# Which partitions the rows of an expert's 64-row block lie in

## The chip, the cores and the metric

One core of one Trainium2 chip. The metric is device time in microseconds (us) of one execution, the median of several. The kernel before takes 1628.13 us (three runs, 1624.47 to 1629.79). TensorE is called PE in the profile, VectorE DVE, ScalarE ACT, GpSimd POOL, SyncE SP; "SPq" and "POOLq" are their instruction queues, where DMAs are issued.

## The reference

Two transformer blocks run one after the other on 512 tokens of width 1024. The first is attention (global and dilated) and a convolutional feed-forward layer, the second a state-space scan beside windowed attention, and then a mixture of experts. Only the mixture matters here:

```python
expert = g_idx * EXPERTS_PER_GROUP + e_idx          # top 2 of 8 experts in the top 1 of 4 groups
...
def expert_block(args):
    xb, e = args
    return (jax.nn.silu(xb @ w_gate[e]) * (xb @ w_up[e])) @ w_down[e]
...
out = jax.ops.segment_sum(y_buf.astype(f32) * w_buf[:, None], tok_buf, num_segments=n_tok + 1)
```

Each of 512 tokens goes to 2 of 32 experts, so an expert has 32 tokens on the average, and which ones is known only on the device. An expert's weights are three matrices of 1024 x 512, 1024 x 512 and 512 x 1024 in float32, 2048 KB each, 6 MB together; 32 experts are 192 MB, all of them read once. The order of an expert's tokens among its rows has no part in the result.

## The kernel before

The mixture of experts begins at about 1036 us (the last norm and the router) and its loop over experts at about 1108 us. The rest of the kernel isn't touched by the change.

**The tables.** The router gives each of the 1024 (token, expert) pairs a block (the expert's own first block of `BLK` = 64 rows, or a later block if it has more than 64) and a rank `pk` in that block, 0 to 63, without gaps. DVE compares `pk` with the constant row `C("place")` (L2223) to make `hot_p`, one column for each partition; PE multiplies it with `hot_b` (L1638), and the product is, for each block and each partition, the number of the token that lies there and its weight (`tok_of`, `place_weight`, L2239 to L2242). A partition in which nobody lies gets an index above the last token.

**The gather.** For expert n, POOL copies column n of `tok_of` to `tok_at` (L916) and issues an indirect DMA (L920). It reads row `tok_at[p]` (4096 bytes) of the normed tokens, which were stored to device memory before, into partition p of `xg`, for the 64 partitions p = 0 to 63. Where the index is out of bounds the row is left out. `xg` has two buffers; the gather of expert n waits until PE has transposed the rows of expert n - 2 out of the same buffer (`xt_filled`), and its rows are wanted at the transposes of expert n, two turns later.

**The turn of an expert.** PE transposes the 64 rows (L1654), DVE scales them (L2249, L2252), PE multiplies by gate and up (L1668, 16 steps over two halves), transposes the hidden rows, and multiplies by down (L1688). The result is split in a high and a low part and added to the tokens by a matmul with a 0/1 matrix `spread` (L1703). `spread` is made by DVE (L2276, L2278): the key of a pair, 64 times its block plus its rank, is compared with `C("slot")`, which says which key a partition holds. All matmul helpers are recorded at L1289, transposes at L1292.

**The weights.** SP streams them through two sets of three slots, `arena` for even and `ring` for odd experts, by one 2048 KB DMA each (`load_expert`, L764). Gate and up of expert n + 2 are issued when PE has done gate and up of expert n; down of expert n + 2 when down of expert n is done. At the time of its issue a load has others ahead of it in the same queue. The loads are all on SP's queue (q1 in the profile), the gathers on POOL's (q0), and both are served by the core's 16 DMA engines. One load is 128 partitions of 16 KB, 8 packets of 16384 bytes for each DMA engine.

Of the kernel before, what the change touches and what calls it, by code (L numbers as in the profile page):

```python
# [14 lines left out]
P = 128  # L15
# [12 lines left out]
BLK = 64  # L28
NOVF = 2 * T // BLK - 1
NBLK = E + NOVF  # L30
# [9 lines left out]
def constants():  # L40

    f = np.float32
    i = np.arange(P)
    col = i[:, None]
    row = i[None, :]
    t = {}
    t["ident"] = np.eye(P, dtype=f)
    t["eps"] = np.full((P, 1), EPS, f)
    t["zero"] = np.zeros((P, 1), f)
    t["upto"] = (col <= row).astype(f)  # L50
    t["from"] = (col >= row).astype(f)
    t["before"] = (col < row).astype(f)
    t["one"] = np.ones((P, 1), f)
    t["window"] = np.concatenate([np.where(row >= col, 0, BIG), np.zeros((P, P)), np.where(row <= col, 0, BIG),
                                  np.zeros((P, CTX))], axis=1).astype(f)
    tok = np.arange(T)
    r, c = (tok // 64).astype(f)[:, None], (tok % 64).astype(f)[:, None]

    def tiles(a):
        return a.reshape(TT, P, -1).transpose(1, 0, 2).reshape(P, -1).astype(f)  # L60

    inv = (f(10000.0) ** (-np.arange(0, 32, 2, dtype=f) / f(32))).astype(f)[None]
    ar, ac = r * inv, c * inv
    rope1 = tiles(np.concatenate([np.cos(ar), np.cos(ar), np.cos(ac), np.cos(ac)], 1)), tiles(np.concatenate(
        [-np.sin(ar), np.sin(ar), -np.sin(ac), np.sin(ac)], 1))
    inv = (f(10000.0) ** (-np.arange(16, dtype=f) / f(16))).astype(f)[None]
    a = np.concatenate([r * inv, c * inv], 1)
    t["cos2"] = tiles(np.concatenate([np.cos(a), np.cos(a)], 1))
    t["sin2"] = tiles(np.concatenate([-np.sin(a), np.sin(a)], 1))
    t["low"] = (i < 64).astype(f)[:, None]  # L70
    t["high"] = (i >= 64).astype(f)[:, None]
    e = np.arange(E)
    t["expert"] = np.tile(e, (P, 1)).astype(f)
    t["group"] = np.tile(e // EG, (P, 1)).astype(f)
    t["blocks_on"] = np.tile(E - 1 - e, (P, 1)).astype(f)
    t["block"] = np.tile(np.arange(NBLK), (P, 1)).astype(f)
    t["place"] = np.tile(np.arange(BLK), (P, 1)).astype(f)
    t["full_blocks"] = np.tile(BLK * np.arange(1, T // BLK), (P, 1)).astype(f)

    t["both_halves"] = (i[:, None] % 64 == np.arange(E + E // EG)[None]).astype(f)  # L80

    t["numbers"] = np.repeat(tok.reshape(TT, P).T + 1, 2, axis=1).astype(f)
    t["slot"] = (np.arange(NBLK)[None] * BLK + (i % BLK)[:, None]).astype(f)
    at, out = {}, []
    for k, v in t.items():
        at[k] = (sum(x.shape[1] for x in out), v.shape[1])
        out.append(v.astype(f))
    return at, np.ascontiguousarray(np.concatenate(out, axis=1)), np.ascontiguousarray(np.concatenate(rope1, axis=1))
# [70 lines left out]
def two_blocks(nc, consts_d, rope1_d, dist_d, h_d, inp, out):  # L159
    ctx = ExitStack()  # L160
    with ctx:
        cols, _, _ = constants()
        ncols = sum(w for _, w in cols.values())

# [2179 lines left out]
```

How the kernel before makes its waits and increments, by code:

```python
    def wait(self, eng, key):  # L112
        eng.wait_ge(self.sem, self.at[key])
# [8 lines left out]
    def link(self, eng, ins):  # L122
        self.n += 1
        ins.then_inc(self.sem, 1)
        eng.wait_ge(self.sem, self.n)
# [26 lines left out]
    def filled(self, eng, key):  # L152
        n = self.at[key]
        eng.wait_ge(self.sems[n % 8], n // 8 + 1)
        return self.banks[n % 8]
# [598 lines left out]
        def load_expert(sp, e, par, kpar, reuse, only=range(3)):  # L754
            for i, (name, pat) in enumerate((("w_gate_2", "a e (p j) f -> (a e) p (j f)"),
                                             ("w_up_2", "a e (p j) f -> (a e) p (j f)"),
                                             ("w_down_2", "a e (p f) d -> (a e) p (f d)"))):
                if i not in only:
                    continue
                kw = {"f": 4} if i == 2 else {"j": KT}
                if reuse is not None:
                    sp.wait_ge(gu_filled if i < 2 else y_filled, reuse)
                sp.dma_start(EXPERT_SLOTS[3 * par + i], inp[name].rearrange(pat, **kw)[e]).then_inc(
                    expert_in[3 * par + i], 16)
# [12 lines left out]
        def columns(sp, first):  # L778
            if first:
                sp.wait_ge(row_stored, 16 * ROWS_BEFORE[6])
                for c in range(2):
                    sp.dma_start(mod[:, c, 0:2, :], h_d[6 * c:6 * c + 2, :].rearrange("s (p j) -> p s j", j=KT)).then_inc(
                        mod_in, 16)
# [4 lines left out]
        @block.sync  # L789
# [36 lines left out]
            route_pe.wait(sp, "halves")
            sp.wait_ge(h_stored, 16)
            sp.wait_ge(expert_in[0], 16)
```

## Time and profile before

| | before |
|---|---|
| median of 3 runs | 1628.13 us |
| profiled execution, its own time | 1627.91 us |
| its span | 1626.1 us |
| PE busy | 1468.7 us (90%) |
| DVE busy | 918.7 us (56%) |
| q1 (SP's DMA queue) | 296.33 MB, 48.8% of 16 engines' span |
| q0 (POOL's DMA queue) | 3200 packets, 7.87 MB, 1.5% |

"Share" of a DMA queue is the time that its packets took, divided by 16 engines times the stretch; it can pass 1 a little, since packets overlap at their ends. In the packet line of the DMA view the counts "under 512 B", "under 2 KB" and "under 8 KB" each hold the ones before. A gathered row is one packet of 4096 bytes, so in a stretch with nothing else of that size the number of rows is the count under 8 KB less the count under 2 KB. A place left empty is a packet of 4 bytes on q0, and so is the end mark of each engine; a gather has 64 + 16 = 80 packets on q0. The end marks of the weight loads are 4-byte packets on q1.

### The profile page before, as it was taken

How to read it: one execution, taken by the hardware profiler on the slowest of the kernel's cores; microseconds unless marked ns; L12 is line 12 of the kernel's file. 1: busy time of each engine (PE TensorE's matmuls, PEld its weight loads, DVE VectorE, ACT ScalarE, POOL GpSimd, SP SyncE). 2: the span in 40 equal slices, each digit the busy share in tenths (PEclk: the TensorE clock that was granted, in tenths of full speed). 3: DMA queues.
4: the chain of work that ended last, by engine and by line, in shares of the span. 5: the costliest groups of instructions: out<-in, count | busy, mean ns of one | idle time of the engine just before them, and what ended most of it. 6: DMA issues, size and time to landing. Idle time of an engine off the chain costs nothing. (4 is left out here: it accounts for less than half of the span.)

```text
span 1626.1 us, 20275 instructions
## 1 busy us (share of the span) xinstructions
PE 1468.7 (90%) x7799; PEld 1018.5 (63%) x7799; DVE 918.7 (56%) x1701; ACT 516.8 (32%) x938; POOL 99.4 (6%) x132
## 2 busy tenths in 40 slices
PE   6899996999999989989998897948998989898896
PEld 5676665788777778877877686734444444343443
DVE  4845774467787667753664676372344344444435
ACT  4435665343353332243426544221111101010102
POOL 0000000000000000001003122001001001000100
PEclk9999997999999999999999998978999999999998
DMA  7222011155444358603010000564999999999993
GB/s 225 78 78 72 1 47 52 52 180 144 140 132 129 95 177 272 209 29 128 26 62 18 1 2 1 207 259 152 406 401 410 416 408 412 398 411 401 410 410 134
DMA packets 103146, 308.33 MB, mean 190 GB/s; under 512 B 12959, under 2 KB 64511, under 8 KB 89739
## 3 DMA queue, kind: packets, MB, share of 16 engines
q1 hardware_dynamic: 93424, 296.33, 48.8%
q0 software_dynamic: 3200, 7.87, 1.5%
q10 hardware_dynamic: 6427, 2.84, 0.7%
q8 instruction: 63, 1.03, 0.3%
q14 instruction: 32, 0.26, 0.1%
HBM read 306.99 MB, written 4.22 MB: 191 GB/s over the span
## 5 line engine op out<-in xcount | busy, mean ns | idle before, releaser
L1289 PE MATMUL bank<-weights_high,hT_high 128*128 128x512 f32 (+2 forms) x736 | 257.6, 388 | 18.6 <-DVE hT_low L1782 5.2
L1289 PE MATMUL bank<-weights_low,hT_high 128*128 128x512 f32 (+2 forms) x560 | 214.8, 384 | 0.0
L1746 DVE TENSOR_TENSOR weights_low<-ring,weights_high 128x2048 fp32r<-128x2048 f32 (+2 forms) x61 | 135.7, 2224 | 137.6 <-ACT weights_high L953 136.7
L953 ACT ACTIVATE weights_high<-ring 128x2048 fp32r<-128x2048 f32 (+2 forms) x61 | 113.4, 1860 | 202.7 <-PE bank L1289 157.2
L1289 PEld LDWEIGHTS bank<-weights_high,hT_high 128*128 128x128 f32 x736 | 140.3, 191 | 47.1 <-issue 11.2
L1289 PE MATMUL bank<-hT_high,weights_high 128*128 128x512 f32 x416 | 164.2, 395 | 1.6 <-DVE hT_low L1784 1.6
L1289 PE MATMUL bank<-hT_low,weights_high 128*128 128x512 f32 x416 | 163.1, 392 | 0.0
L1289 PE MATMUL bank<-hT_high,weights_low 128*128 128x512 f32 x416 | 161.8, 389 | 0.0
L2249 DVE TENSOR_TENSOR hTc<-bank,mod_gain 128x512 f32<-128x512 f32 x32 | 22.1, 691 | 229.2 <-PE bank L1292 229.2
L1289 PE MATMUL bank<-arena,hTc 128*64 128x512 f32 x496 | 117.7, 614 | 21.8 <-DMA arena<-in_w_up 20.2
L1289 PE MATMUL bank<-ring,hTc 128*64 128x512 f32 (+1 forms) x544 | 120.8, 582 | 13.3 <-DMA ring<-in_w_up 13.3
L1289 PEld LDWEIGHTS bank<-weights_low,hT_high 128*128 128x128 f32 x560 | 106.9, 191 | 20.4 <-issue 0.2
L1289 PEld LDWEIGHTS bank<-ring,hTc 128*64 128x64 f32 (+1 forms) x544 | 46.5, 140 | 86.1 <-issue 85.0
L1289 PEld LDWEIGHTS bank<-arena,hTc 128*64 128x64 f32 x496 | 42.1, 141 | 91.5 <-issue 91.5
L1292 PEld LDWEIGHTS bank<-const,xn 64*128 64x128 f32 (+1 forms) x464 | 62.3, 203 | 57.9 <-issue 45.7
L1292 PE MATMUL bank<-const,xn 64*128 64x64 f32 (+1 forms) x464 | 67.7, 301 | 30.6 <-DVE xn L1766 19.6
L1289 PEld LDWEIGHTS bank<-hT_high,weights_high 128*128 128x128 f32 x416 | 78.2, 188 | 22.1 <-issue 3.4
L1256 ACT ACTIVATE hTc<-bank 128x512 f32<-128x512 f32 x32 | 19.1, 597 | 222.6 <-PE bank L1289 222.6
L1289 PEld LDWEIGHTS bank<-hT_high,weights_low 128*128 128x128 f32 x416 | 78.1, 188 | 17.3
L1292 PE MATMUL bank<-const,arena 128*128 128x128 f32 x429 | 71.5, 294 | 18.7 <-ACT arena L1072 6.2
L1289 PEld LDWEIGHTS bank<-hT_low,weights_high 128*128 128x128 f32 x416 | 78.1, 188 | 16.4
L1289 PE MATMUL bank<-weights_high,hT_low 128*128 128x512 f32 (+1 forms) x224 | 85.3, 381 | 0.0
(324 smaller groups left out, 2328.4 us busy)
## 6 DMA issues: line engine op xcount, KB each, us to landing
arena<-in_w_up SPq DMA_DIRECT2D x16, 2048.0 KB, 23.3
arena<-in_w_down SPq DMA_DIRECT2D x16, 2048.0 KB, 21.6
ring<-in_w_gate SPq DMA_DIRECT2D x16, 2048.0 KB, 18.4
ring<-in_w_up SPq DMA_DIRECT2D x16, 2048.0 KB, 23.5
ring<-in_w_down SPq DMA_DIRECT2D x16, 2048.0 KB, 22.4
arena<-in_w_gate SPq DMA_DIRECT2D x15, 2048.0 KB, 18.2
xn<-in_w_ada SPq DMA_DIRECT2D x48, 512.0 KB, 5.0
ring<-in_w_up SPq DMA_DIRECT2D x44, 512.0 KB, 5.1
```

The lines of the kernel that those rows point to most:

```text
L953: high_ready.tick(s.activation(part_view(w_high, key), raw_view(key), ACT.Copy), k)
L1256: s.activation(gu[:, par, :], ps[1][:, :], ACT.Copy).then_inc(gu_ready, 1)
L1289: return nc.tensor.matmul(o, lhsT, rhs, start=start, stop=stop)
L1292: return nc.tensor.transpose(o, i, ident[0:n, 0:n])
L1746: low_ready.tick(v.tensor_tensor(part_view(w_low, key), raw_view(key), part_view(w_high, key), ALU.subtract), k)
L2249: v.tensor_tensor(xT[:, par, :, :], ps[0][:, :].rearrange("p (j n) -> p j n", j=KT), wide(mod_gain[:, 2, :], BLK), ALU.mult).then_inc(xt_s ...
```

## The change

Only constants change. `held[p]` is the rank that partition p holds. Before it is p itself; now it is 16 (p mod 4) + p // 4. So rank r lies in partition 4 (r mod 16) + r // 16: ranks 0 to 15 in partitions 0, 4, 8, ... 60, ranks 16 to 31 in 1, 5, ... 61, and so on. `place` (which rank a partition takes when the table is made) and `slot` (which key a partition has when results are spread) both follow it, so each row is still found where it lies. No instruction, shape or wait is added, removed or moved.

```diff
-    t["place"] = np.tile(np.arange(BLK), (P, 1)).astype(f)
+    held = np.arange(BLK) % 4 * (BLK // 4) + np.arange(BLK) // 4
+    t["place"] = np.tile(held, (P, 1)).astype(f)
...
-    t["slot"] = (np.arange(NBLK)[None] * BLK + (i % BLK)[:, None]).astype(f)
+    t["slot"] = (np.arange(NBLK)[None] * BLK + held[i % BLK][:, None]).astype(f)
```

## Rows read from the trace of the kernel before

**Rows 1.** Waits in 1110 to 1600 us: who waited for whom: us in total, times, longest
```profile
PE bank L1289 <- DMA arena<-in_w_up: 20.2, 12, 3.1
PE bank L1289 <- DMA ring<-in_w_up: 13.3, 11, 2.0
```

**Rows 2.** The chain that ended last, in order of time: start us, us, what
```profile
1178.29 12.50 PE bank L1289 x64
...
1192.50 12.53 PE bank L1289 x64
...
1205.62 23.20 DMA arena<-in_w_up
...
1571.64 21.60 DMA ring<-in_w_up
...
1593.38 7.10 PE bank L1289 x32
```

**Rows 3.** Busy time by stretch; the last two numbers are DMA share and GB/s
```profile
1110.00:1150.00 40.00, 37.61 (x166) 14.68 (x166) 9.33 (x16) 3.90 (x8) 3.56 (x6) 0.89 0.70 263
1150.00:1205.00 55.00, 55.00 (x293) 23.56 (x291) 26.41 (x43) 5.77 (x11) 5.38 (x7) 1.00 1.01 407
1205.00:1400.00 195.00, 177.86 (x939) 82.66 (x940) 83.53 (x136) 20.32 (x38) 18.03 (x26) 0.99 1.01 409
```

**Rows 4.** The same view where the weight stream runs out
```profile
1576.00:1578.00 2.00, 2.00 (x12) 0.57 (x8) 1.54 (x3) 0.00 (x0) 0.00 (x0) 1.00 1.00 426
...
1588.00:1590.00 2.00, 2.00 (x18) 1.15 (x16) 1.94 (x5) 0.00 (x0) 0.00 (x0) 1.00 0.92 393
1590.00:1592.00 2.00, 2.00 (x13) 0.59 (x10) 1.97 (x4) 0.00 (x0) 0.00 (x0) 1.00 0.81 344
1592.00:1594.00 2.00, 1.63 (x10) 0.52 (x8) 0.95 (x2) 0.16 (x1) 0.00 (x0) 1.00 0.52 221
1594.00:1596.00 2.00, 2.00 (x12) 0.72 (x10) 0.69 (x1) 0.47 (x1) 0.00 (x0) 1.00 0.31 131
```

**Rows 5.** DMA view, 1126.1 to 1127.5 us (queue: packets, MB, share of 16 engines)
```profile
DMA packets 114, 0.39 MB, mean 278 GB/s; under 512 B 73, under 2 KB 73, under 8 KB 96
...
q0 software_dynamic: 80, 0.09, 18.8%
```

**Rows 6.** DMA view, 1448.84 to 1449.25 us: the first 0.41 us of a gather
```profile
DMA packets 19, 0.16 MB, mean 400 GB/s; under 512 B 3, under 2 KB 3, under 8 KB 11
...
q0 software_dynamic: 11, 0.03, 20.4%
```

**Rows 7.** DMA view, 1450.50 to 1454.0 us: the later part of that gather
```profile
DMA packets 137, 1.39 MB, mean 398 GB/s; under 512 B 52, under 2 KB 52, under 8 KB 52
```

**Rows 8.** DMA view, 1448.84 to 1453.5 us: that gather whole
```profile
DMA packets 196, 1.75 MB, mean 376 GB/s; under 512 B 74, under 2 KB 74, under 8 KB 94
```

**Rows 9.** DMA view, a larger gather: 1496.82 to 1498.85, then 1498.85 to 1501.3
```profile
DMA packets 77, 0.66 MB, mean 327 GB/s; under 512 B 11, under 2 KB 11, under 8 KB 45
...
DMA packets 96, 0.85 MB, mean 348 GB/s; under 512 B 38, under 2 KB 38, under 8 KB 46
```

**Rows 10.** DMA view, 1496.82 to 1501.9 us: the same gather whole
```profile
DMA packets 190, 1.78 MB, mean 350 GB/s; under 512 B 50, under 2 KB 50, under 8 KB 92
...
q0 software_dynamic: 80, 0.17, 10.4%
```

**Rows 11.** DMA view, 1384.0 to 1389.5 us: the largest gather
```profile
DMA packets 187, 1.79 MB, mean 325 GB/s; under 512 B 36, under 2 KB 36, under 8 KB 92
```

**Rows 12.** DMA view, first and last of 26 gathers: from 1168.8, from 1561.1, 5.5 us each
```profile
DMA packets 222, 2.15 MB, mean 391 GB/s; under 512 B 78, under 2 KB 78, under 8 KB 95
...
DMA packets 213, 2.04 MB, mean 370 GB/s; under 512 B 73, under 2 KB 73, under 8 KB 94
```

**Rows 13.** The instructions on token_index
```profile
L920 POOL DMA_INDIRECT xn<-normed_tokens,token_index x32: 962/1207/1281, 1103.3 to 1556.8; - x32
...
DMA to landing us min/median/max: 3.1/8.9/9.8
```

## The prediction

> **What bounds the kernel now.** I read the waits of the loop over experts first [rows 1]. PE waits for the up weights 23 times, 33.5 us in all, and for no other DMA. The chain in order of time says from when [rows 2]: up to about 1205 us it is PE's own work, a turn of 14.2 us for an expert (1178.29 to 1192.50), and from 1205.62 on it goes from one up load to the next, until the last one lands at 1593.24. From the issue at 1205.62 to the issue at 1571.64 there are 366.0 us for 23 experts, 15.91 us each. So in this stage DMA is the bound, and PE, which needs 14.2 us, has 1.7 us to spare in each turn. The view by stretches agrees [rows 3]: DMA share 1.01 from 1150 us on. With one load in service and more in the queue, an engine always has its next packet.
>
> The question is then which DMA engine. A load has landed when the last of 16 engines is done, and each engine has its own eight packets of it. Where the stream runs out, the engines do not stop together [rows 4]: the rate is still 426 GB/s at 1576 us, and the share falls to 0.92, 0.81, 0.52, 0.31 over 8 us and isn't at zero by 1596. The same bytes were given to each of them, so some engines had come 8 us and more ahead of the last. The missing share in these four stretches is 0.16 + 0.38 + 0.96 + 1.38 = 2.9 us, and some 1.5 more behind 1596 (over 0.69 missing, for about 2 us): the mean engine is about 4.4 us ahead of the slowest, and the slowest alone sets the pace. What differs between engines is what they carry for the gathers.
>
> **The ledger of a turn.** At 426 GB/s an engine moves 26.6 GB/s, so a packet of 16384 bytes takes 0.615 us, and 24 packets 14.76 us. A gathered row costs an engine, where little else runs, 0.16 us: 18.8% of 16 x 1.4 us is 4.2 us for 80 packets, of which 23 are rows (96 - 73) [rows 5]. Next to weights the row's packet took 0.20 us (10.4% of 16 x 5.08 us = 8.5 us over 42 rows) [rows 10], but then everything is slower, and time given to a row is time not spent on a slowed weight packet. I take 0.16 and keep 0.20.
> Beside this, a gather slows all weight packets for a while. At 426 GB/s the 4.66 us of one gather [rows 8] would carry 1.99 MB and carried 1.75: 0.56 us lost for 20 rows. The 5.08 us of another [rows 10]: 2.16 against 1.78 MB, 0.90 us for 42 rows. The 5.5 us of the largest gather [rows 11]: 2.34 against 1.79, 1.29 us for 56. That is 0.028, 0.021 and 0.023 us a row, about in proportion to the rows. (The row's own bytes are in the MB, at the full rate, so this is slowing alone.) With 32 rows it is some 0.75 us a turn. 14.76 + 0.75 leaves 0.40 of the 15.91 us for the slowest engine's own rows, 2.5 at 0.16.
>
> **How places are dealt to engines.** Between two packets of q0 an engine serves a weight packet (0.615 us or more), so turns can be counted. In the gather of 20 rows [rows 6 to 8], 3 of the first 11 packets of q0 are already empty places, in 0.41 us, in which no engine can have had a second turn, while 12 rows had not begun. So places don't go to the engines one by one (20 rows would give each of 16 engines a row first). And by 1450.50, 1.66 us after the start, all rows have begun (52 - 52 = 0 later), which is two turns, so no engine has four. Two rows on ten engines and none on six fits. In the gather of 42 rows [rows 9] 34 rows begin in the first two turns' time and 8 after it: about 32, then 10. I conclude: engine e serves partitions 2e and 2e + 1, then 32 + 2e and 33 + 2e.
>
> **The change part by part.**
> Tables, comparisons, matmuls, transposes: same instructions on same shapes, other values: 0.
> Rows by engine. Before, with n rows up to 32, engine 0 has 2; with 34 or more it has 4. After, rank r lies in partition 4 (r mod 16) + r // 16; halved and mod 16 that is engine 2 (r mod 8) for the ranks 0 to 31, so all of them go to the eight even engines, and 32 and up to the odd ones. Engine 0 has 3 rows for n from 17 to 24, and 4 from 25 on. I read n from the DMA view of each of the 26 gathers from 1168.8 us on (first 95 - 78 = 17, last 94 - 73 = 21) [rows 12]: 7 have 17 to 24 rows, 9 have 25 to 31, 10 have 37 to 56, 831 rows in all. Engine 0 before: 16 x 2 + 10 x 4 = 72. After: 7 x 3 + 9 x 4 + 10 x 4 = 97. The mean engine has 51.9 both times. Before, the busiest is 20 rows above the mean, 3.2 us at 0.16, of the 4.4 us by which the slowest lags [rows 4]; so the deal explains most of the lag that is there, and I take it that engine 0 or its neighbour is the slowest.
> Added: 25 rows x 0.16 = 4.0 us on the engine that sets the pace (5.0 at 0.20; 0 if the pace is set elsewhere). Nothing hides it: PE's 1.7 us to spare in a turn is on the other side, and the even engines never run dry. The light engines get further ahead, which gives nothing back.
> The first gathers, before 1168.8 us, fall where DMA isn't the bound (share 0.70, then PE's chain) [rows 2, 3]. The very first is waited for; with 34 rows or more it has four on engine 0 either way, with fewer it has two more, 0.3 us. I take 0.
> Landing of a gather: 8.9 us now, at most 9.8 [rows 13]. Every engine takes five turns of q0 either way, empty or not; two more of them with a row are 0.4 us, and the rows are wanted two turns (31.8 us) after the wait that frees the buffer. Hidden; it would cost only if 20 us of cover went.
> The slowing of all packets: by the rows above it follows the number of rows, which stays. I take 0. From below: half as many rows at a time could slow less than in proportion, at most half of 26 x 0.75 = 19.5 us, -9.8. From above: the thinnest gather is the dearest per row (0.028 against 0.022), and the change thins all: 831 x 0.006 = +5.0.
> Sum: 4.0 us. The profiled execution took 1627.91 us, 0.2 under the median; so 1631.9, and 1632.1 as a median.
>
> The Trainium skill has another deal. "DMA: Bandwidth & Descriptors", section "The descriptor swizzle", puts groups of four neighbouring partitions on an engine, and partitions 0 to 63 on eight engines (for a transfer to 128 partitions). By that rule the change would spread the rows better and save time, and the forecast would change its sign. Rows 6 to 8 disagree for this 64-place gather: an engine would need at least four turns for 20 rows, and two were enough. It is the second rival below.
>
> **The rivals.**
> *Thin is dear.* As in the bound above: rows spread over twice the turns slow the weights longer. 4.0 + 5.0 = 9.0 us, 1637.1. For it: 0.028 at 20 rows. Against: 0.021 at 42, 0.023 at 56, where the later turns are thin too.
> *Faster, by the deal.* Fours of neighbours on 16 engines: engine 0 has four rows in every gather before (104), and afterwards 2, 3 or 4 (64): -40 x 0.16 = -6.4, 1621.7. Eights (four and four) on 8 engines: 144 before, 115 after, -4.6, 1623.5. Decides if the counted turns of rows 6 to 9 are misread.
> *Faster, by the crowd.* The slowing is caused by rows in flight together, and halves: 4.0 - 9.8 = -5.8, 1622.3. Against: proportional so far.
> *No change.* The slowest engine is another one, slow by something besides rows and odd-numbered or with few of them; it stays the slowest, and 4.4 us of lag cover the added rows: 1628.
>
> **How the numbers follow.** 0.3% is 4.9 us, about what a measurement of this kernel can tell from no change. Forecast 0.52 (own range 1630 to 1635.5; 0.16 of it over 1633.0). Thin is dear 0.20 (0.19 slower). Faster by the deal 0.06 (0.05). Faster by the crowd 0.08 (0.07). No change 0.14 (0.01 slower). Slower 0.16 + 0.19 + 0.01 = 0.36, faster 0.12, the same 0.52. The range takes in most of the first rival above and the unchanged kernel below, 1626 to 1638.
>
> **What would show it.** PE waits for up loads again 23 times or a few more, with 33.5 + 4 us or so; 366 us from 1205.62 to the last issue become 370. The stream's end is longer drawn out: share falls earlier, near half for a while (odd engines done, even ones not). A gather of 20 rows has rows in its third turn, past 1.66 us. Up to 1205 us nothing moves. If the end gets shorter and the rate in the stage goes up, the deal was read wrongly; if the loss in a gather of 20 rows moves from 0.56 us, the slowing depends on the crowd.

## The result and the profile after

The changed kernel takes 1633.97 us (median of 19 runs, 1629.11 to 1638.74) against 1628.27 us (19 runs, 1624.05 to 1636.63): 5.7 us more between the medians, ratio 1.0028 with a 95% interval of 1.0016 to 1.0040 (2.6 to 6.5 us). Forecast were 1632.1 us and +4.0.

It is the loop over experts that grew. Helpers stand one line lower, since the change adds a line. The view by tile has the gate and up multiplies with their first and last start: first the kernel before, then the changed one.

```profile
L1289 PE MATMUL bank<-ring,hTc x512: 592/592/643, 1126.1 to 1599.9; 128*64 128x512 f32 x171
L1289 PE MATMUL bank<-arena,hTc x496: 592/592/1112, 1109.8 to 1585.1; 128*64 128x512 f32 x166
```

```profile
L1290 PE MATMUL bank<-ring,hTc x512: 592/592/1061, 1125.7 to 1604.2; 128*64 128x512 f32 x171
L1290 PE MATMUL bank<-arena,hTc x496: 592/592/1112, 1107.7 to 1589.6; 128*64 128x512 f32 x166
```

From the first of them to the start of the last: 1599.9 - 1109.8 = 490.1 us before, 496.5 after. I call this the stage. Second traces of both (below) gave 491.3 and 494.7, so the means are 490.7 and 495.6: +4.9 us, and a single trace is good to 1 or 2 us. What lies before the stage differs from trace to trace as well (the first multiply started at 1107.7 to 1117.7 us in the traces of this study), by more than the change is worth; the stage is the sharper measure.

The waits of the changed kernel in 1110 to 1600 us answer to [rows 1]: 24 instead of 23, 36.3 us instead of 33.5.

```profile
PE bank L1290 <- DMA arena<-in_w_up: 19.6, 13, 2.4
PE bank L1290 <- DMA ring<-in_w_up: 16.7, 11, 2.3
```

Its chain of waits, in order of time, as [rows 2]: the same alternation of an up load and PE, to a last landing at 1597.60 instead of 1593.24.

```profile
1204.15 24.79 DMA arena<-in_w_up
1229.08 7.10 PE bank L1290 x32
1236.77 24.50 DMA arena<-in_w_up
...
1575.80 21.80 DMA ring<-in_w_up
...
1597.74 7.10 PE bank L1290 x32
```

The end of the stream, by stretches, the last two columns DMA share and GB/s, as [rows 4]:

```profile
1592.00:1594.00 2.00, 2.00 (x18) 1.37 (x18) 1.94 (x4) 0.29 (x1) 0.00 (x0) 1.00 0.56 238
1594.00:1596.00 2.00, 2.00 (x10) 0.63 (x10) 1.97 (x5) 0.00 (x0) 0.00 (x0) 1.00 0.48 205
1596.00:1598.00 2.00, 1.77 (x10) 0.51 (x8) 1.14 (x2) 0.00 (x0) 0.00 (x0) 1.00 0.48 205
1598.00:1600.00 2.00, 2.00 (x12) 0.78 (x10) 1.00 (x2) 0.63 (x1) 0.00 (x0) 1.00 0.37 156
1600.00:1602.00 2.00, 2.00 (x12) 0.77 (x10) 0.00 (x0) 0.00 (x0) 0.00 (x0) 1.00 0.12 49
```

Before, the share fell in a slope. Now it stands at 0.48 of 16 engines, 8 of them, for 4 us: one half is done, the other isn't. The trace also keeps the 16 landings of each load, one for each engine. Those of the last up load are at 1587.02 to 1588.84 us for eight engines and at 1593.79 to 1597.61 for the other eight; before, they lay without such a gap from 1583.41 to 1593.24. That is the deal that the prediction read from the counts.

The same gather of 20 rows, in the DMA view: its first 0.41 us (from 1452.95), what comes after 1.66 us (from 1454.61, 3.5 us long), and 4.66 us whole; compare [rows 6 to 8].

```profile
DMA packets 22, 0.19 MB, mean 460 GB/s; under 512 B 6, under 2 KB 6, under 8 KB 12
...
DMA packets 131, 1.38 MB, mean 396 GB/s; under 512 B 42, under 2 KB 42, under 8 KB 48
...
DMA packets 201, 1.82 MB, mean 390 GB/s; under 512 B 75, under 2 KB 75, under 8 KB 95
```

Six rows (48 - 42) begin after 1.66 us where none did. A gather of 28 rows shows it better: rows begun in its first 1.66 us and after, in the kernel before (from 1367.79 us) and in the changed one (from 1373.43).

```profile
DMA packets 64, 0.54 MB, mean 328 GB/s; under 512 B 12, under 2 KB 12, under 8 KB 37
...
DMA packets 134, 1.29 MB, mean 385 GB/s; under 512 B 53, under 2 KB 53, under 8 KB 56
```

```profile
DMA packets 76, 0.61 MB, mean 365 GB/s; under 512 B 27, under 2 KB 27, under 8 KB 43
...
DMA packets 124, 1.23 MB, mean 371 GB/s; under 512 B 40, under 2 KB 40, under 8 KB 52
```

25 and 3 rows before, 16 and 12 after: four turns instead of two.

One more reading serves all kernels: how far the weight packets are slowed. In 1150 to 1575 us the q1 row gives packets, MB and share. Before: 97.8% of 425 us is 415.7 us per engine; 169.30 MB are 10,333 weight packets, 646 an engine, 396.5 us at 0.614 us (what a weight packet takes with no gather by). The difference, 19.1 us, is the slowing. (This stretch holds 27 gathers, one of 17 rows ahead of the 26 that the prediction counts: 848 rows in all.) First the kernel before (two traces), then the changed one (two traces):

```profile
q1 hardware_dynamic: 11736, 169.30, 97.8%
...
q1 hardware_dynamic: 11747, 169.55, 97.9%
```

```profile
q1 hardware_dynamic: 11657, 168.12, 97.8%
...
q1 hardware_dynamic: 11659, 168.19, 97.7%
```

19.1 and 19.0 us before, 21.9 and 21.3 after: +2.6 us (a tenth of a per cent of the share is 0.4 us, and two traces of one kernel differ by 0.1 and 0.6).

### The profile page after: what moved, and what is told of

Read it like the earlier page. It is cut to its first block and busy times, and to the rows that moved or that the text cites. A ratio compares the mean times of both kernels' runs of the same rounds, so it can differ in the third digit from the quotient of the medians.

```text
span 1630.2 us, 20275 instructions
## 1 busy us (share of the span) xinstructions
PE 1471.8 (90%) x7799; PEld 1020.0 (63%) x7799; DVE 918.3 (56%) x1701; ACT 516.1 (32%) x938; POOL 99.5 (6%) x132
## 5 line engine op out<-in xcount | busy, mean ns | idle before, releaser
L1257 ACT ACTIVATE hTc<-bank 128x512 f32<-128x512 f32 x32 | 19.1, 597 | 228.9 <-PE bank L1290 228.9
L1293 PE MATMUL bank<-const,arena 128*128 128x128 f32 x429 | 68.4, 285 | 18.8 <-ACT arena L1073 6.8
## 6 DMA issues: line engine op xcount, KB each, us to landing
ring<-in_w_gate SPq DMA_DIRECT2D x16, 2048.0 KB, 18.8
ring<-in_w_down SPq DMA_DIRECT2D x16, 2048.0 KB, 22.8
xn<-in_w_ada SPq DMA_DIRECT2D x48, 512.0 KB, 4.7
ring<-in_w_up SPq DMA_DIRECT2D x44, 512.0 KB, 5.3
```

The lines of the kernel that those rows point to most:

```text
L1257: s.activation(gu[:, par, :], ps[1][:, :], ACT.Copy).then_inc(gu_ready, 1)
L1293: return nc.tensor.transpose(o, i, ident[0:n, 0:n])
```

## The experiments

In the table "busiest" is the most rows that an engine has in the 26 gathers by the deal in pairs. The expectations of the last four runs count the stage to the first multiply of the last expert, 6.5 us sooner (483.6 us for the kernel before); the table counts as above. Only the ratio has an interval; stage and slowing are from one trace each, two for the first two. In all_64_rows and fours, which are slower, the stretch of the slowing holds one gather fewer (26), so theirs is some 0.7 to 1.1 us too low in comparison.

| kernel | busiest | rows | stage us | slowing us | ratio to before (95%) |
|---|---|---|---|---|---|
| before | 72 | 831 | 490.7 | 19.1 | 1.0003 (0.9984 to 1.0022) |
| changed | 97 | 831 | 495.6 | 21.6 | 1.0028; again 1.0038 (1.0021 to 1.0056) |
| fill_engine0 | 104 | 863 | 492.6 | 19.2 | 1.0018 (0.9997 to 1.0039) |
| fill_engine15 | 73 | 883 | 492.9 | 21.8 | 1.0017 (0.9999 to 1.0036) |
| all_64_rows | 104 | 1664 | 512.0 | 29.8 | 1.0161 (1.0131 to 1.0191) |
| no_rows | 0 | 0 | 459.6 | 2.3 (to 1550 us) | 0.9816 (0.9786 to 0.9846) |
| even_ranks | 64 | 831 | 488.3 | 18.1 | 0.9989 (0.9970 to 1.0008) |
| even_ranks_apart | 64 | 831 | 487.1 | 18.2 | 0.9987 (0.9966 to 1.0009) |
| snake | 56 | 831 | 488.4 | 18.8 | 0.9999 (0.9977 to 1.0020) |
| fours | 104 | 831 | 502.7 | 22.8 | 1.0068 (1.0043 to 1.0093) |
| thin_16_engines | 64 | 831 | 489.5 | 20.3 | 1.0005 (0.9986 to 1.0025) |
| one_row_for_all | 72 | 831 | 488.4 | 17.9 | 1.0009 (0.9986 to 1.0031) |

**More rows, same order.** The first four kernels keep the order of the kernel before and change what empty places, or all places, read:

```diff
-            link(v.tensor_scalar(tval, numbers, 0.0, 16384.0, ALU.is_equal, ALU.mult))
+            link(v.scalar_tensor_tensor(tval, numbers, 0.0, C("filler"), ALU.is_equal, ALU.mult))
...
+    other = (np.arange(NBLK)[None] * 37 + i[:, None] * 101) % T + 1
+    t["filler"] = np.where(np.isin(i, (0, 1, 32, 33))[:, None], other, 16384).astype(f)
```

(`(62, 63)` for the second, `i < 64` for the third; for no_rows `is_ge` in place of `is_equal` in the old line.)

> The order of ranks is that of the kernel before; the empty places in partitions 0, 1, 32 and 33 (those of engine 0 by the deal in pairs) are given real rows, so engine 0 has 104 rows in the 26 gathers instead of 72, 32 rows more of 831. Theory (the engine with the most rows sets the pace, 0.16 us a row, and each row slows all packets by 0.023 us): 32 x 0.16 + 32 x 0.023 = +5.9 us over the kernel before. Rival (only the number of rows counts, by the slowing of all): +0.7 us. Rival (the pace is set by another engine, for instance one that fetches instructions): +0.7 to +2 us.

+1.9 us in the stage, +0.18% in time, with an interval that reaches no change. The 32 rows on engine 0 cost a third of the expected, and the slowing didn't move.

> As the run on engine 0, but the places filled are partitions 62 and 63, of the engine that has fewest rows: 21 + 52 = 73 in the 26 gathers, 52 rows more in all. Theory: the most is 73 instead of 72, so +0.2 us own and 52 x 0.023 = 1.2 us of slowing, +1.4 us. Rival (only the number counts): more than the run on engine 0, by 52 to 32.

+2.2 us in the stage, +0.17%. The two can't be told apart by their times. But here the slowing rose by 2.7 us and is as large as the whole cost, while on engine 0 it rose by 0.1. That is 0.05 us for each of these 52 rows, twice the 0.023 of the prediction, and next to nothing for each of the 32 on engine 0, though those too were the only rows of their turns. So lone rows as such aren't shown to be dear.

> All 64 places of each gather carry a real row (the empty ones one that nobody uses): 1664 rows in the 26 gathers instead of 831, 104 on each engine instead of at most 72. Theory: 32 x 0.16 = 5.1 us own and 833 x 0.023 = 19.2 us of slowing, +24 us over the kernel before. Rival (thin is dear: a full crowd costs little more per turn than a thin one): own 5.1 and half of 19.2, some +15 us. The landings of a load over the 16 engines should lie close together, since all carry the same.

+21.3 us in the stage, +1.61% (26 us): nearer to the theory's 24 than to the rival's 15, but not for its reasons. The slowing rose by 10.7 us, 0.013 a row: a full crowd is cheap per row, as the rival says. The rest, 10.6 us, is twice the 5.1 us that the theory gave engine 0; the paragraph on single engines below says where it comes from. The landings of the last up load lie 5.8 us apart, against 9.8 before: closer, but not together.

> No gather brings a row (all indices are out of bounds; the tokens of the expert layer are left out). What stays is 24 weight packets a turn, 14.8 us, still more than PE's 14.2. Theory: 72 x 0.16 = 11.5 us own and 831 x 0.023 = 19.1 us of slowing go, -30 us; at least -26, since PE's own turn becomes the bound in part of the stage. Rival (the lag between engines has another cause than rows): the landings of a load stay spread over 8 us or more, and only some 20 us go.

-31.1 us in the stage, -1.84% (30 us; 25 to 35): as expected. So all gathers together cost 30 us of 1628, though the profile's page gives q0 1.5% of 16 engines' span. Without rows the engines still don't end together. Stretches at the end of this kernel's stream:

```profile
1556.00:1558.00 2.00, 2.00 (x12) 0.69 (x8) 0.00 (x0) 0.00 (x0) 0.00 (x0) 1.00 0.96 397
...
1566.00:1568.00 2.00, 1.81 (x10) 0.81 (x12) 1.30 (x2) 0.63 (x1) 0.00 (x0) 1.00 0.67 287
1568.00:1570.00 2.00, 2.00 (x12) 0.79 (x10) 0.00 (x1) 0.00 (x0) 0.00 (x0) 1.00 0.21 90
1570.00:1572.00 2.00, 2.00 (x12) 0.86 (x10) 0.00 (x0) 0.00 (x0) 0.00 (x0) 1.00 0.00 0
```

The fall takes about half as long as in [rows 4]: the landings of the last up load lie 4.9 us apart, against 9.8 before. A part of the lag isn't from rows.

**Same rows, other orders.** The next four have only another table:

```diff
-    held = np.arange(BLK) % 4 * (BLK // 4) + np.arange(BLK) // 4
+    k = np.arange(BLK)
+    held = k // 32 * 32 + k % 2 * 16 + k % 32 // 2                                     # even_ranks
+    held = k % 2 * 32 + k // 32 * 16 + k % 32 // 2                                     # even_ranks_apart
+    held = k % 32 // 2 * 4 + k // 32 * 2 + k % 2                                       # fours
+    held = k // 32 * 32 + np.where(k % 2 == 0, k % 32 // 2, 31 - k % 32 // 2)          # snake
```

> Ranks dealt to the engines one by one: rank r (under 32) in partition 2 (r mod 16) + r // 16, the rest alike from partition 32 on. Engine 0 then has 64 rows in the 26 gathers instead of 72 before and 97 in the changed kernel; turns 1 and 2 carry the ranks under 32. Theory: -8 x 0.16 = -1.3 us against the kernel before, -5.3 against the changed one. Rival (the change is slower because rows are spread thinly over turns, not by the sum on an engine): the same as before, since ranks under 32 take two turns as before.

-2.4 us in the stage, ratio 0.9989. The sign is the theory's; in time it isn't separated from no change.

> The same 64 rows at most on an engine, but the second sixteen ranks lie in the partitions from 32 on, so that an engine serves a row, an empty place, a row, an empty place: turns 1 and 3. Theory (sum on an engine, slowing in proportion to rows): as the run with ranks one by one, -1.3 us against before. Rival (thin is dear: rows spread over more turns slow the weights longer): slower than that run by 831 x 0.006 = 5 us at most, +3.7 against before.

-3.6 us, slowing 18.2 against 18.1. A gap between the two turns costs nothing that shows; sixteen rows are still under way together in each.

> Ranks 0 to 3 on engine 0, 4 to 7 on engine 1 and so on: engine 0 has four rows in every gather, 104 in the 26, engines 14 and 15 none. Theory: 32 x 0.16 = +5.1 us against the kernel before (+1.1 against the changed one), and more if spreading over four turns slows the weights, as the changed kernel's trace suggests (+2 to +3): +5 to +8. Rival (the most rows on an engine doesn't matter): 0.

+12.0 us in the stage, +0.68% (7 to 15 us): more than the 5 to 8 expected, though the interval reaches them. It has the same busiest sum as fill_engine0, 104, and takes 10 us more, 3.6 of them by slowing. The end of its stream says where more lies (stretches of 2 us):

```profile
1606.00:1608.00 2.00, 2.00 (x16) 0.91 (x14) 1.94 (x5) 0.00 (x0) 0.00 (x0) 1.00 0.29 123
...
1610.00:1612.00 2.00, 1.83 (x10) 0.57 (x8) 0.75 (x1) 0.63 (x1) 0.00 (x0) 1.00 0.06 25
1612.00:1614.00 2.00, 2.00 (x12) 0.86 (x10) 0.69 (x1) 0.00 (x0) 0.00 (x0) 1.00 0.08 33
```

A share of 0.06 is one engine of 16, alone for some 5 us, though four engines have 104 rows each. The landings of the last up load say the same: 12 engines by 1602.15 us, three from 1604.78 to 1605.78, one at 1610.57. Something besides rows holds this one back. By fill_engine0 it is probably not engine 0; what it is stays open.

> Ranks 0 to 15 forwards over the 16 engines and 16 to 31 backwards (then 32 to 47 forwards, 48 to 63 backwards): the sums over the 26 gathers lie between 46 and 56, though a single gather still has up to 2, 3 or 4 rows on an engine as with ranks one by one. Theory (the sum over the stage counts, since the queue never runs dry): -16 x 0.16 = -2.6 us against the kernel before. Rival (each gather's busiest engine counts, 64 in sum): -1.3 us, as ranks one by one. The spread of a load's landings over the engines should be the smallest of all kernels.

-2.3 us in the stage, ratio 0.9999: no better than ranks one by one. Evening out the sums below 64 brings nothing that shows. It can't decide between the sum over the stage and each gather's busiest engine. The landings of the last up load lie 6.0 us apart, less than in any other kernel with 831 rows (7.1 to 10.6), as expected.

**Second traces, thin rows, one address.**

> The kernel before once more, for a second trace of it. Every theory: the time of the kernel before, and from the first gate and up multiply to the last 483.6 us as in the first trace, within 1 to 2 us; this says how far single traces of this stage can be told apart.

491.3 us in the stage, slowing 19.0; ratio 1.0003.

> The changed kernel once more on the chip of these runs, for a second trace. Every theory: +4 to +6 us over the kernel before, 490 us from the first gate and up multiply to the last.

494.7 us, slowing 21.3, ratio 1.0038. The change's cost stands a second time.

```diff
+    e, late, odd = k % 32 // 2, k // 32, k % 2
+    held = e + 16 * odd + 32 * (late != e % 2)                                         # thin_16_engines
```

> As thin as the changed kernel and as even as ranks one by one: even engines take their ranks under 32 in turns 1 and 2, odd engines in turns 3 and 4, so that some 8 rows are under way in a turn, in four turns, yet no engine has more than 64 rows in the 26 gathers. Theory (the sum on the busiest engine): as ranks one by one, 482 us in the stage, -1.3 us against before. Rival (rows few at a time slow the weights more, which would be the part of the change's cost that its rows on one engine don't explain): the weights' slowing rises as in the changed kernel, 485 us in the stage, +1.5 us against before.

The slowing is 20.3 us, against 18.1 and 18.2 for the two even kernels, at the same sums. Here are the q1 rows in 1150 to 1575 us of the thin kernel, then of even_ranks:

```profile
q1 hardware_dynamic: 11696, 168.79, 97.8%
```

```profile
q1 hardware_dynamic: 11748, 169.53, 97.7%
```

So most of the change's added slowing seems to come from few rows at a time over four turns (2.2 of the 3.5 us between even_ranks and the changed kernel), not from their being on one half of the engines. This rests on one trace, where repeats differ by up to 0.6 us. In the stage it is +1.2 us (489.5 against 488.3), and the ratios overlap: its worth in time is not shown.

```diff
-            v.scalar_tensor_tensor(tok_of[:, :], numbers, -1.0, tval, ALU.add, ALU.add)
+            v.scalar_tensor_tensor(tok_of[:, :], numbers, 0.0, tval, ALU.mult, ALU.add)
```

> Placement of the kernel before, but all places that hold a token read token 0's row, so the expert layer works on one token (its values are left out). As many rows, packets and engines as before; only the addresses read differ. Theory (the slowing beside a gather has nothing to do with where in memory the rows are read): 483.6 us in the stage, +0. Rival (scattered reads from device memory are what slows the weights): the slowing falls or rises by much, -10 us or more, or +10 with all engines at one address.

-2.3 us in the stage, ratio 1.0009, slowing 17.9 against 19.1. Where the rows are read from matters little; what slows the weights comes with any row.

**What single engines carry.** The views sum over the engines, but the packet records of a trace can be sorted by engine: a packet begins 3 to 4 ns before the recorded end of the one before it on its engine (93% of them in the kernel before, nearly all in no_rows), so the packets link up in 16 chains, one for each engine. In all_64_rows each chain has 104 rows; in the kernel before they have 72 down to 21, as the deal in pairs has it. Two neighbouring chains may have been swapped here and there, so counts in the middle are good to a few rows. The chains show a load that neither the prediction nor the table above has: instruction packets of 16 KB on q8, about 1.05 us each. The kernel before, 1150 to 1575 us:

```profile
q8 instruction: 16, 0.26, 0.3%
```

They fall on some nine of the engines, mostly two on each. (Six more on q14, of 8 KB and 0.3 us each, are left aside here.) The table has the time, in us, at which the last weight packet of a chain ended; "instruction packets" are those of q8.

| kernel | chain | end |
|---|---|---|
| no_rows | nine with instruction packets | 1568.5 to 1570.4 |
| no_rows | seven without | 1565.6 to 1567.1 |
| all_64_rows | 104 rows, three instruction packets | 1624.1 |
| all_64_rows | 104 rows, none (eight chains) | 1618.3 to 1621.9 |
| before | 60 rows, three instruction packets | 1597.64 |
| before | 71 rows, none | 1597.57 |
| before | 72 rows, none | 1595.51 |
| before | 58 rows, two instruction packets | 1595.07 |
| before | 21 rows, none | 1587.91 |
| fill_engine0 | 104 rows | 1598.54 |
| fill_engine0 | 60 rows, three instruction packets | 1597.18 |
| fill_engine0 | 21 rows, none | 1588.61 |

So the lag without rows goes with the instruction packets. In the kernel before, an engine with only 60 rows was last, level with one of 71 (in the second trace it ended at 1599.14, two chains of 72 rows at 1599.80 and 1597.92). In all_64_rows the last chain has three instruction packets again, so it is this engine, with 44 rows more; its rows took 21.0 us instead of 12.3, which is most of the unexplained 10.6. And a row costs its engine somewhat less than its packet takes: 72 rows against 21 end 7.6 us apart, 0.15 a row; 104 against 21 in fill_engine0 9.9 us, 0.12 a row.

## Why the prediction was right, and where not

*PE isn't the bound, the up loads are, and one engine sets the pace.* Right: the chain is the same, and the tail shows engines in two halves. Only "one" is too strong: in the kernel before two engines ended level.

*The deal in pairs.* Right, by the counts of 28 rows (25 and 3 against 16 and 12), the 0.48 plateau and the 104 rows on every engine in all_64_rows. The rival with fours or eights of neighbours would have made the change faster; the ratio's interval excludes that. The section "The descriptor swizzle" of the page "DMA: Bandwidth & Descriptors" in the Trainium skill gives its deal for a transfer to 128 partitions; this gather to 64 doesn't follow it. One step of the counting was loose: between two packets of q0 an engine often serves a 4-byte end mark of q1 (246 of some 2080 times in the kernel before) instead of a weight packet, so a turn can be much shorter than 0.615 us. The conclusion stands by the other counts.

*25 rows x 0.16 = 4.0 us on the engine that sets the pace.* The size came near by luck. Of 4.9 us in the stage 2.6 are slowing, so some 2.3 are left for rows, not 4.0. The step that failed is "engine 0 or its neighbour is the slowest". The neighbour was, but level with the engine of 60 rows and three instruction packets, for which the prediction has no term; by the deal that is engine 5, an odd one, and the change takes it from 60 rows to 16. Engine 0 was 2.1 us ahead of both. That is why 32 more rows on it cost 1.9 us: at 0.12 to 0.15 a row they are 3.8 to 4.8 us, less the 2.1 that it was ahead. For the change an estimate in the same way: engine 6 (58 rows, two instruction packets) ended 2.6 us ahead of the last and got 35 rows more, 4.2 to 5.3 us, which makes 1.6 to 2.7; with 2.6 of slowing that is 4.2 to 5.3, and 4.9 were measured. Engine 2 (ended at 1596.6, 24 rows more) comes to about the same, 1.9 to 2.6; engine 0, with 25 more, to 0.9 to 1.7. In the second trace of the changed kernel the two chains that end last (1605.9 and 1605.7) carry two instruction packets each, and the chain of 97 rows ends at 1603.6. The excess of fours over this account stays open.

*The slowing: 0.* Wrong by 2.6 us. It was kept as the rival "thin is dear", bound +5.0. The thin kernel and all_64_rows bear that rival out: 0.013 us a row for the places that all_64_rows fills, 0.022 on the average before, and 2 us more where the same rows come over four turns. Of the kernels with lone rows one fits (fill_engine15, 0.05 a row) and one doesn't (fill_engine0, 0.1 us for 32), so what exactly makes a row dear stays open. The evidence in the prediction (proportional at 20, 42 and 56 rows) compared gathers that all begin with one crowd of up to 32. Nor does every gather show it: the one of 20 rows lost 0.40 us after (1.99 against 1.82 MB) and 0.56 before; only the sum over the stage does.

The two errors, too much for the rows of the slowest engine and nothing for the slowing, cancel in part, so the sum was near: 4.0 forecast, 4.9 in the stage, 4.6 by the ratio. *Hidden landing, first gathers, tables: 0.* Nothing in the traces speaks against it.

Against both kernels the best orders (ranks one by one, together or apart) measure 0.9989 and 0.9987 of the kernel before, with intervals that reach over 1, and 0.4% below the changed one.

## What to carry to other kernels

Where a stage waits for loads spread over 16 DMA engines, count what the busiest engine carries besides; the mean and the queue's share of time hide it (1.5% on the profile's page, 30 us in fact). Read the deal of places to engines from the trace of that very transfer before choosing an order: a table that would even out the rows under the deal for 128 partitions (144 to 115 in the prediction's rival) made them more uneven under the true one (72 to 97). And before adding to an engine, find out whether it is the last one: look at the 16 landings of a load, and at what else the engines carry, instruction packets too.

## What the runs showed of the hardware

- A gather of 64 places by indirect DMA gave each engine two neighbouring partitions, and two more 32 further on. A row of 4096 bytes took its engine 0.16 us with little beside it and 0.20 beside the weights; by where engines ended, it set its engine back by 0.12 to 0.15 us.
- While rows are under way all weight packets are slowed, also those of engines without a row: 19 us for 848 rows (0.022 a row), less for rows added to a full crowd (0.013), and hardly dependent on the address (17.9 us with all rows at one). In the kernel before the weight packets of the engine with 21 rows took 0.644 us in the mean, those of the engine with 72 rows 0.640.
- With no rows at all, engines that serve the same weight packets still end up to 4.9 us apart over the stage. The nine that also carry instruction packets (one to three of 16 KB, about 1.05 us each) are the late ones.
- A place left empty is a packet of 4 bytes that takes its engine 0.009 us.
